# A 17-stage float32 kernel: first weights of five stages loaded one stage ahead, and experts in four lanes for two

## The reference, cut to what matters

```python
# hyena
p = h @ w_in
u = short_conv(p[..., :3 * 1024], conv_w, conv_b)      # three taps
gate = p[..., 3 * 1024:]
for o in range(2):
    z = parts[o + 1] * long_conv(z, k_f[:, o], skip[o])
y = (z * silu(gate)) @ w_out
# mixture of experts: 16 experts, 2 per token
y[tok] += g * ((silu(xb @ w1[e]) * (xb @ w3[e])) @ w2[e])   # w1, w3 1024x512, w2 512x1024
```

## Time and profile before

| | us |
|---|---|
| median of three runs | 5146.45 |
| the profiled execution | 5143.57 |
| its span, first to last instruction | 5141.9 |
| PE busy | 4357.6 (85%) |
| DVE busy | 1922.3 (37%) |
| ACT busy | 1159.5 (23%) |
| POOL busy | 278.6 (5%) |
| attention, first to last PE work | about 556 to 1203 |
| hyena projection | 1364 to 1928 |
| long convolution | 1937 to 2537 |
| ho | 2539 to 2692 |
| even projection | 2694 to 3028 |
| eo | 3228 to 3385 |
| route and blocks, layer 0 | 3386 to 4016 |
| route and blocks, layer 1 | about 4475 to 5099 |

### The profile page before, as it was taken

The page is one execution under the profiler, slowest core; times in us unless marked ns, Lnnn a source line. Parts: engine busy times, 40 slices in busy tenths (PEclk is TensorE's granted clock), DMA queues, the critical chain, the costliest instruction groups (busy, mean ns, idle before and its releaser), DMA issues. The chain is left out here.

```text
span 5141.9 us, 52299 instructions
## 1 busy us (share of the span) xinstructions
PE 4357.6 (85%) x17971; PEld 2236.7 (43%) x17971; DVE 1922.3 (37%) x2999; ACT 1159.5 (23%) x1920; POOL 278.6 (5%) x390
## 2 busy tenths in 40 slices
PE   3699799997799997999589978859999599779995
PEld 1354455554344445777444445423333244333332
DVE  1233444443222104998546647221111423411113
ACT  0122354442111012222020336101111244111111
POOL 0100000000000000111000000000000200000001
PEclk7899899998899997999799989979999799989998
DMA  6322221113344412111231120447653511266745
GB/s 246 112 64 74 53 49 36 35 35 120 153 153 171 185 56 77 51 51 50 98 108 60 46 78 21 152 170 291 233 210 136 183 42 41 94 259 235 277 183 207
DMA packets 262066, 629.15 MB, mean 122 GB/s; under 512 B 74045, under 2 KB 153997, under 8 KB 242489
## 3 DMA queue, kind: packets, MB, share of 16 engines
q1 hardware_dynamic: 219314, 497.53, 27.7%
q0 software_dynamic: 21856, 102.40, 5.3%
q10 hardware_dynamic: 20776, 27.64, 1.5%
HBM read 899.85 MB, written 117.73 MB: 198 GB/s over the span
## 5 line engine op out<-in xcount | busy, mean ns | idle before, releaser
L3348 PE MATMUL blocks_h<-moe_w,blocks_xT 128*64 128x512 f32 x3072 | 689.1, 602 | 35.6 <-ACT blocks_xT L3290 15.6
L3348 PEld LDWEIGHTS blocks_h<-moe_w,blocks_xT 128*64 128x64 f32 x3072 | 222.4, 139 | 458.1 <-issue 453.2
L1611 PE MATMUL hyp_acc<-hy_hT,hyp_weights 128*128 128x512 f32 x768 | 337.8, 599 | 27.6 <-DMA hyp_weights<-in_hy_w_in 27.6
L3369 PE MATMUL blocks_acc<-moe_w,blocks_hidT 128*64 128x512 f32 x1536 | 340.1, 595 | 1.6 <-DVE blocks_hidT L3253 1.6
L969 PE MATMUL att_scores<-att_kT,att_qT 64*128 64x512 f32 (+3 forms) x768 | 252.2, 549 | 20.9 <-DMA att_v<-scratch_V 20.9
L700 PE MATMUL lat_acc<-lat_w_in,lat_hT 128*128 128x512 f32 (+1 forms) x640 | 244.2, 537 | 4.2 <-DMA lat_w_in<-in_attn_w_in 4.2
L2151 PE MATMUL evp_acc<-ev_hT,evp_weights 128*128 128x512 f32 x512 | 227.5, 606 | 10.5 <-DMA evp_weights<-in_ev_in_w 4.6
L1611 PEld LDWEIGHTS hyp_acc<-hy_hT,hyp_weights 128*128 128x128 f32 x768 | 146.3, 193 | 204.3 <-issue 204.3
L905 DVE TENSOR_REDUCE att_nmax<-att_scores 128x1 f32<-128x1280 f32 x128 | 190.2, 1486 | 101.6 <-PE att_scores L969 101.6
L993 PE MATMUL att_turn<-ident,att_probs 128*128 128x128 f32 x1280 | 192.9, 281 | 41.5 <-DVE att_o L935 22.6
L873 ACT ACTIVATE att_probs<-att_scores,att_nmax 128x1280 f32<-128x1280 f32 x128 | 169.9, 1327 | 173.9 <-DVE att_nmax L905 171.9
(11 more groups left out here) (520 smaller groups left out, 5931.8 us busy)
## 6 DMA issues: line engine op xcount, KB each, us to landing
moe_w<-in_ex_w SPq DMA_DIRECT2D x288, 2048.0 KB
hyp_m_weights<-in_mod_w POOLq DMA_DIRECT2D x6, 8192.0 KB, 24.1
mod_weights<-in_ada_w SPq DMA_DIRECT2D x6, 4096.0 KB, 23.2
scratch_y_rows<-blocks_y ACTq DMA_DIRECT2D x48, 512.0 KB, 8.5
hyp_weights<-in_hy_w_in SPq DMA_DIRECT2D x8, 2048.0 KB, 27.4
scratch_parts<-hyp_uT SPq DMA_DIRECT2D x24, 512.0 KB, 3.3
evp_weights<-in_ev_in_w SPq DMA_DIRECT2D x5, 2048.0 KB, 12.7
lat_w_in<-in_attn_w_in SPq DMA_DIRECT2D x4, 2048.0 KB, 19.3
```

The source lines that it names most:

```text
L1611: mm = nc.tensor.matmul(acc[:, m % 2, half * NC:(half + 1) * NC], weights[:, ws, kt, c:c + P], hT[:, kt, half * NC:(half + 1) * NC], start ...
L3348: mm = nc.tensor.matmul(out[mine, :], xT[:, s, kt, mine], w[:, l, kt, :], start=(kt == 0), stop=(kt == KT - 1))
L3369: mm = nc.tensor.matmul(acc[mine, c, :], hidT[:, kt, mine], w2[:, l, kt, c * NC:(c + 1) * NC], start=(kt == 0), stop=(kt == FT - 1))
```

## The change

- `weights_ahead`, `hyena_weights`, `even_weights` and `Filter` allocate the first weights (and taps, and the convolution's tables) outside their stage; the stage before loads them on SP: attention for ao, ao for the hyena projection, the hyena projection for the long convolution, ho for the even projection, stick-breaking for eo. Their semaphores are cleared by the stage that loads them. ho's own weights stay where they are. In `project_out` the loads for the next stage stand after the gain row and before the loop.
- In `project_out` the columns' gain (and eo's fold) is made after back(0,0), by `prepare`; ACT waits for it in `write_out`.
- In the hyena projection a third's last turn comes after the next third's first product; behind the last third the first gate product comes before the last turn. The gate is stored by SP. DVE sums w3 at the end of this stage.
- LANES is 4, so MB is 32 and STEPS is 20. Four lanes of w1, w3 and w2 need hT as room for two lanes of w1; xT, y and the hidden rows have one buffer for two; the Silu writes where the product is formed and so waits for the turn of the step before. The route's large temporaries lie in the last lane's w2, whose first load waits for the token table. The combine's rows lie in w3 and w1's second half. The descriptor scratch of the program is 8192 bytes per partition.

The diff, cut to its core:

```diff
@@ -843,6 +843,7 @@
...
                 pairs(sp, body)
+                ahead[0](sp)
...
@@ -1087,6 +1088,8 @@
...
     back(0, 0)
+    if prepare is not None:
+        prepare()
...
@@ -1125,7 +1128,31 @@
...
+def weights_ahead(nc, ctx, tag, w):
...
+    sb, _, sem, _ = tools(nc, ctx, f"{tag}_early")
+    weights, w_in = out_weights(sb, sem)
+
+    def load(sp):
+        for c in range(2):
+            load_out_weights(sp, w, weights, w_in, c)
+
+    return (weights, w_in), (load, w_in)
...
@@ -1201,10 +1227,10 @@
...
                 for c in range(2):
...
-                    sp.dma_start(weights[:, :, c * NC:(c + 1) * NC], wv[:, :, c * NC:(c + 1) * NC]).then_inc(w_in[c], 16)
+                    if early is None:
+                        load_out_weights(sp, w, weights, w_in, c)
...
@@ -1213,6 +1239,8 @@
...
+                if ahead is not None:
+                    ahead[0](sp)
...
@@ -1279,6 +1307,7 @@
...
                     act.wait_ge(h_turned, signals(n * S + (s + 1)))
+                    act.wait_ge(gain_ready, signals(1))
...
@@ -1346,18 +1374,20 @@
...
-                    dve.wait_ge(cols_in, signals(48))
-                    nc.vector.scalar_tensor_tensor(h_gain[:, :], cols[:, 1, :], 1.0, cols[:, 2, :], ALU.add,
-                                                   ALU.mult).then_inc(gain_ready, 1)
-                    dve.wait_ge(gain_ready, signals(1))
+                def prepare():
...
-                    three_parts(dve, TT, front, gates, norm_rows, back, write_out)
...
+                    three_parts(dve, TT, front, gates, norm_rows, back, write_out, prepare)
...
@@ -1493,18 +1519,25 @@
...
-                for s in range(2):
-                    load(0, s)
+                load_filter(sp, d, conv)
...
+                for t in range(TT):
+                    for s in range(2):
+                        sp.wait_ge(gated, signals(2 * t + s + 1))
+                        sp.dma_start(d["gate1"][t * P:(t + 1) * P, s * NC:(s + 1) * NC], gate[:, s, :]).then_inc(gate_out[s], 16)
...
@@ -1526,12 +1559,6 @@
...
-                for t in range(TT):
-                    for s in range(2):
-                        pool.wait_ge(gated, signals(2 * t + s + 1))
-                        pool.dma_start(d["gate1"][t * P:(t + 1) * P, s * NC:(s + 1) * NC], gate[:, s, :]).then_inc(gate_out[s], 16)
...
@@ -1598,6 +1625,13 @@
...
+                dve.wait_ge(conv.w3_in, signals(16 * 10))
+                fw, bw = w3[:, :, 0, :], w3[:, :, 1, :]
+                nc.vector.tensor_tensor(fw, fw, bw, ALU.add).then_inc(conv.w3_sums, 1)
...
@@ -1631,27 +1665,82 @@
...
-                with pe.Fori(0, HY_PARTS) as i:
-                    multiply(i, 0)
+
+                def rest(i):
                     for m in range(1, CH_TILES):
                         multiply(i, m)
                         if m % HALF_TILES == HALF_TILES - 1:
                             modulation(i, m // HALF_TILES)
                         turning(i, m - 1)
+
+                multiply(0, 0)
+                with pe.Fori(0, HY_PARTS - 1) as i:
+                    rest(i)
+                    multiply(i + 1, 0)
                     turning(i, CH_TILES - 1)
-                pe.wait_ge(conved, signals(NQ + 2))
-                for s in range(2):
-                    pe.wait_ge(w_in[s], signals(16 * (HY_PARTS + 1)))
+                rest(HY_PARTS - 1)
                 for t in range(TT):
                     for s in range(2):
-                        pe.wait_ge(gated, signals(2 * t + s - 1)) if t else None
+                        if t:
+                            pe.wait_ge(gated, signals(2 * t + s - 1))
+                        else:
+                            pe.wait_ge(conved, signals(NQ + 1 + s))
+                            pe.wait_ge(w_in[s], signals(16 * (HY_PARTS + 1)))
...
+                        if t == 0 and s == 0:
+                            turning(HY_PARTS - 1, CH_TILES - 1)
...
+def hyena_weights(nc, d, ctx):
...
+    def load(sp):
+        sp.dma_start(tap_rows[0:TAPS * rows, :], d["hy_conv_w"][0].rearrange("j (q p) -> (j q) p", p=P)).then_inc(taps_in, 16)
...
+        for s in range(2):
+            sp.dma_start(weights[:, s, :, :], wv[:, :, s * NC:(s + 1) * NC]).then_inc(w_in[s], 16)
...
+def load_filter(sp, d, conv):
...
+    for o in range(2):
+        for v in range(2):
+            sp.dma_start(conv.w3[0:HY_FFN, o * QP:(o + 1) * QP, v, :], w3v[o, v]).then_inc(conv.w3_in, 16)
...
+    sp.dma_start(conv.hid[0:HY_FFN, :, :], d["hid"].rearrange("k (t p) -> k t p", p=P)).then_inc(conv.w3_in, 16)
+    sp.dma_start(conv.negt[:, :], d["k_negt"]).then_inc(conv.w3_in, 16)
+    sp.dma_start(conv.deltas[:, :], row(d["k_deltas"][0:CCH], P)).then_inc(conv.deltas_in, 16)
+    sp.dma_start(conv.fwd[:, :, :, :, :], d["k_fwd"]).then_inc(conv.mats_in, 16)
...
@@ -1971,13 +2046,6 @@
...
-                    dve.wait_ge(w3_in, signals(16 * 11))
...
-                    tt(fw, fw, bw, ALU.add).then_inc(w3_sums, 1)
-                    nc.vector.tensor_scalar(bw, bw, -2.0, None, ALU.mult).then_inc(w3_sums, 1)
-                    dve.wait_ge(w3_sums, signals(2))
-                    tt(bw, fw, bw, ALU.add).then_inc(w3_sums, 1)
...
@@ -2115,11 +2177,7 @@
...
-                sp.dma_start(tap_rows[:, :], d["ev_dw_w_2"][0]).then_inc(taps_in, 16)
-                load(1, 1)
-                load(0, 0)
                 sp.dma_start(bias[:, :], columns(d["ev_dw_b_2"][0]), allow_slow_non_contiguous=True).then_inc(bias_in, 16)
-                load(2, 2)
...
+def even_weights(nc, d, ctx):
...
+    def load(sp):
+        sp.dma_start(tap_rows[:, :], d["ev_dw_w_2"][0]).then_inc(taps_in, 16)
+        wv = d["ev_in_w_2"][0].rearrange("(kt p) n -> p kt n", p=P)
+        for c in (1, 0, 2):
+            sp.dma_start(weights[:, c, :, :], wv[:, :, c * NC:(c + 1) * NC]).then_inc(w_in[c], 16)
...
@@ -2931,7 +3006,7 @@
...
-LANES = 2
+LANES = 4
...
@@ -2972,11 +3047,14 @@
...
-        ended, row_block = sb("ended", [P, TT * TOP, PLACES]), sb("row_block", [P, TT * TOP])
...
+        at_place = room[:, 0:at_size].rearrange("p (j b) -> p j b", b=P)
+        ended, row_block = room[:, at_size:at_size + ended_size].rearrange("p (j b) -> p j b", b=PLACES), sb("row_block", [P, TT * TOP])
...
@@ -2992,7 +3070,7 @@
...
                 sp.wait_ge(owned, signals(1))
-                load_first(sp)
+                load_first(sp, tabled)
...
@@ -3102,6 +3180,8 @@
...
                 link(ts(lane[:, :], row_block[:, :], float(STEPS), None, ALU.is_ge))
+                for l in range(2, LANES):
+                    link(stt(lane[:, :], row_block[:, :], float(l * STEPS), lane[:, :], ALU.is_ge, ALU.add))
...
@@ -3128,15 +3208,15 @@
...
-        x, xT = sb("x", [P, S, D]), sb("xT", [P, S, KT, P])
-        act1, hid = sb("act1", [P, FF]), sb("hid", [P, FF])
+        x, xT = sb("x", [P, S, D]), sb("xT", [P, KT, P])
+        hid = sb("hid", [P, FF])
         hidT = sb("hidT", [P, FT, P])
-        y = sb("y", [P, S, D])
+        y = sb("y", [P, D])
...
@@ -3191,11 +3271,10 @@
...
+                    up_weights(t + 1, next_experts(t + 1))
+                    down_weights(t, next_experts(t))
+                down_weights(STEPS - 1, next_experts(STEPS - 1))
+                sp.wait_ge(h1_made, signals(STEPS))
...
@@ -3232,9 +3311,9 @@
...
-                        dve.wait_ge(h3_made, signals(b - 1))
+                        dve.wait_ge(h3_made, signals(b))
...
@@ -3243,8 +3322,7 @@
...
-                    dve.wait_ge(hid_turned, signals(b))
-                    nc.vector.tensor_tensor(hid[:, :], act1[:, :], h3[:, :], ALU.mult).then_inc(gated, 1)
+                    nc.vector.tensor_tensor(hid[:, :], hid[:, :], h3[:, :], ALU.mult).then_inc(gated, 1)
...
@@ -3285,32 +3363,32 @@
...
+                    act.wait_ge(hid_turned, signals(b))
...
@@ -3578,32 +3654,45 @@
...
+        w1b, w3_all = sb("w1b", [P, KT, D]), sb("w3", [P, LANES, KT, FF])
+        w1 = [halves(a[:, h * FT:(h + 1) * FT, :]) for a in (room, w1b) for h in range(2)]
+        w3 = [w3_all[:, l, :, :] for l in range(LANES)]
...
+            def load_first(sp, tabled):
+                each = [sp.value_load(owners[0:1, l * STEPS:l * STEPS + 1], min_val=0, max_val=EXPERTS - 1) for l in range(LANES)]
+                for m, dst in enumerate((w1, w3, w2)):
+                    for l in range(LANES):
+                        if (m, l) == (PARTS - 1, LANES - 1):
+                            sp.wait_ge(tabled, signals(1))
+                        load_part(sp, d, layer, dst[l], m, each[l]).then_inc(w_in[l][m], 16)
...
@@ -3680,32 +3769,40 @@
...
-        stage_attention(nc, d, ident)
...
-        stage_long_conv(nc, d)
...
+        with ExitStack() as outer:
+            conv = Filter(nc, outer)
+            with nc.sbuf_tensor("hy_hT", [P, KT, L], F32) as hT, ExitStack() as inner:
+                hyp_early, hyp_ahead = hyena_weights(nc, d, inner)
+                with ExitStack() as inmost:
```

(10 more changed lines are left out.)

238 lines of the change are left out of this document (121 added, 117 removed).

## The result

The median went from 5147.73 us to 4975.65 us (4973.66 to 4982.96), a ratio of 0.9669 with an interval of 0.9654 to 0.9685. The prediction was 4966, range 4938 to 5022. The profiled execution has a span of 4972.0 us, so the two spans differ by 169.9.

The account below looks back on a forecast made before the run. PE binds inside the stages and DMA at their borders. Experts -102.3 us, the other terms from ao to eo together with ho's +12, sum -180.1 against the profiled 5143.57: 4963.5, with 2.9 for the median 4966, range 4938 to 5022.

Parts of the forecast that it names:

- Experts, the pace: Expert stages: a step stays at 22.67 us with four lanes, so four fewer steps give -90.7 us per layer.
- time per record: Rival, expert products: the doubled records each carry time of their own, +248 us, 5214; chance 0.04.
- lanes only in pairs: Rival, expert products: groups with different stationary data overlap two at a time, +845 us, 5811; chance 0.02.
- Experts, the start: Before each layer's first expert product: norm columns wait behind 25.17 MB and tables grow, +30.9 us per layer.
- the lower end: Start of the experts: columns and weights come in time, +1.8 us per layer against the expected +30.9.
- Experts, the changes: Expert steps with two lanes changing: one more stall per layer, +3 us each; layer 1's last down product, +7.3.
- PE idle in expert steps where no two lanes change: Expert steps: a sign that would show the prediction wrong; stalls were expected only where two lanes change.
- Hyena: Hyena projection, first to last product: two waits for hyp_u go, a gate product runs ahead, -15.7 us.
- ho: ho's third turn: a and g land 16 us later behind the next stage's loads, PE waits 11.5 us, +12 in all.
- no stall in ho: Rival: ho has no stall, and hyena's end gains -7.3 us, 4951, inside the range; chance 0.12.
- The other borders: Hyena's start -29.3 us, ao -8.4, eo -7.6, gate stores -4, convolution's start -15.4, even projection -9.4.
- DMA-bound steps: Rival, expert steps: DMA at 342 GB/s, an expert takes 18.4 us, a double 36.8, time 5026; chance 0.13.

Follow-up runs that it names:

- The columns' run: Changed kernel with the blocks' norm columns loaded by SP in the route stage, ahead of the twelve expert weight loads: 4930.57 us.
- the run without crossing: Changed kernel with PE's hyena order as before: a third's last turn ahead of the next third's first product, gate products behind both weight halves: 4989.84 us.
- the two runs: Changed kernel with the even projection's weights queued in ho behind the loop's first pass, 4973.46 us, or behind the whole loop, 4956.21 us.

## Why the prediction was right, point by point

**Experts, the pace: right.** 22.64 us for 22.67, with twice the records per product. The rivals *time per record* and *lanes only in pairs* needed products over 7.1 us, and are out. The overhead per matmul that the Trainium skill gives (TensorEngine Tiling (Array Packing), Instruction Overhead) doesn't show: my estimate from it was 96 us, and the steps of four lanes are shorter by 0.03 us each than those of two.

**Experts, the start: right in cause, 2.1 us too low in layer 0.** From the route's first product to the blocks' first it is 79.4 us for 46.4, so +33.0, against +30.9. Of that 2.8 are the tables ahead of the first issue (1.8 predicted). The columns' run shows that the wait is theirs. It also shows the lower end (+1.8, columns and weights in time) to be out of reach: of what the columns' place gave, 5.7 us went again in layer 0, and 18 in the second step of layer 1, which the prediction hadn't looked at.

**Experts, the changes: right in place, too small in size.** This is the step that failed most, "one such stall more per layer: +3 each". Between first and last product layer 0 took 563.2 us before and 482.3 after, -81.0, where -90.7 + 3 = -87.7 was said: +9.7 for the changes and not +3. In layer 1 what came ahead of the last down product cost +10.5. One late step costs 5.7 to 7.0 us and not 3. Its idle time is 3.7 to 5.3 us, where the prediction worked out 2 to 3, and all but one of the products behind it are 1.3 to 2.7 us slower, which it had at nothing. It took the stalls of before at about 3 too, though they cost 3.5 to 8.4. Of the +10.5, 2.5 are layer 1's second step, late by PE's wait of 2.41 us for the w1 of a single lane. "PE idle in expert steps where no two lanes change" was one of the prediction's own signs of being wrong: it holds in this one step, and w1 stood there behind the first loads. These sizes are those of one execution. In the profiles of the five kernels whose expert code is that of the changed kernel, first to last product takes 478.2 to 482.6 us in layer 0 and 482.2 to 489.5 in layer 1, so the +9.7 may be some 4 less. The last down product of layer 1 is 9.02 us late and then takes 9.96 for 7.07, together 11.9, of which 0.8 was idle before as well, against +7.3. The combine pays 5 of that back, since the residual's load, which otherwise ends the stage, runs beside the wait: the stage closed 4.6 us after its last product, 9.5 in layer 0.

**Hyena: 5.8 us more than said, in part for the same reason.** The prediction let two idle times of 4.29 us go and one product of 7.07 us run ahead of the gate's weights. In the profile all three waits for hyp_u are gone, and the wait for the gate's weights is 3.13 us for 4.78, so 14.5 us of idle time went. The other 7.0 of the 21.5 us is time in products; the windows of the run without crossing show them at 0.50 behind such gaps. That run has the idle times back, and 21.5 us with them.

**ho: right, +15.4 for +12.** The stall sat where it was said to sit, ahead of the third turn, 15.11 us long for 11.5: counted from ho's first product, DVE has the next g at 28.8 us (2507.91) and not at 10.0, so 18.8 later, where 16 was said. The rival *no stall in ho* is out, and the two runs show that the queue's order is all of it.

**The other borders: right within 3 us.** Hyena's start -30.1 for -29.3, ao -9.6 for -8.4, eo -7.1 for -7.6. At the convolution's start 21.7 for 19.4. Ahead of the stage's first instruction 6.4 us went (11.0 to 4.6), where -4 was said within 0 and -7.3; the stores' change of queue is 2.25 of it, and the rest is open. From there to PE's first product 15.3 went (15.5 to 0.2), which is the -15.4 of the tables and sums loaded ahead. The even projection gained 11.6 for 9.4.

**DMA-bound steps: out in this kernel.** In both layers the steps without a double change are 22.64 us from the third on. The rival was right on one thing, the limit itself: with doubles in all steps the pace is DMA's, but at 428 GB/s and not at 342.

The errors go both ways: experts 14.6 us less gain than said, the borders and the crossing up to the convolution's first product 10 more. So the sum was better than its largest terms, and that it came within 10 us of the measured time is in part luck.

## What to carry to other kernels

Count idle time of PE at more than its length: here most gaps of 2.2 to 5 us cost another 1.3 to 3 in slow matmuls behind them, though not all. When a stage loads ahead for the next one, put those loads behind the last load that the running stage itself needs, not at the first free moment, and put few small bytes that gate the start ahead of the many large ones. After taking a wait away, look one step further for the load that was hidden by it.
